# One inference step of a hybrid encoder layer: two dot or value half points in place of a whole point, 96 places of block 1 beside the mixers and 32 before them

## The chip, the cores and the metric

The kernel runs on one core of one Trainium2 chip. The metric is the device time of one execution in microseconds; lower is better.

## What is computed

One layer over nine blocks of 128 rows: block 0 holds 8 running streams of 16 frames, blocks 1 to 8 one new stream of 1024 frames. Cut to what matters:

```python
h = rmsnorm(x)                                        # D_MODEL = 1024
qa, ka, va, qb, kb, vb, rg, ga, gb = project(h)       # one product with w_in, 5888 columns
oa = softmax(qa @ ka + alibi, with sinks) @ va        # mixer A: 8 heads, own block and the one before
ob = norm(retention(qb, kb, vb, state)) * silu(rg)    # mixer B: 4 heads, state carried from block to block
x1 = x + (sigmoid(ga) * (oa @ w_a) + sigmoid(gb) * (ob @ w_b)) @ w_out
h2 = rmsnorm(x1)
q = h2 @ w_q; idx, gate = top16 of 128 x 128 product keys, for each of 8 heads
# 128 experts for each row, out of 16384; each has a row u and a row v of 1024 numbers
y = rmsnorm(x1 + sum_k gate_k * gelu(h2 . u[idx_k]) * v[idx_k])
```

The outputs are y of all rows, the newest keys and values, and the states.

## The kernel before

All is float32. **Stages** follow one another with a barrier between them, since each has buffers of its own.

1. The projection of blocks 0 and 1; the mixers of block 0; the mixers of block 1.
2. The projection stage. TensorE multiplies blocks 2 to 8 with the weights, in 16 tiles of columns; ScalarE scales each result into `zo` and stores it as `z_d`. Beside it VectorE searches the experts of blocks 0 and 1, and works off all 128 places of block 0 and the first `AHEAD` = 48 of block 1. A **place** is one expert for each of the 128 rows. It needs a gather of u rows (512 KB), a dot product with `h2` (one instruction over 1024 columns), later a gather of v rows and a weighted sum into the accumulator. The rows land in a ring of 16 slots; `ORDER1` is the order of 16 u or v rows each for block 1. At the end the accumulator is stored to `ac_d`.
3. The mixer stage, blocks 2 to 8. Beside the mixers VectorE works off the other places of block 1, here 80.
4. The last stage: the experts of blocks 2 to 8. Here u and v rows come with one gather, from a **table** `uv_d` of 16384 x 2048 numbers in memory. The kernel itself copies peer_u and peer_v into it, in 128 parts with two copies of 512 KB each (`pool_table`), by GpSimd's queue, at most two parts in flight: 24, 22 and 16 parts in stage 1, 20 ahead of the gathers in stage 2 (`TABLE_E` = 62 to `TABLE_S` = 82), and the other 46 in the mixer stage, two after each group of gathers from block 3 on.

**Order in the mixer stage.** Each engine has one list of instructions, written by hand, and works it off in order. Block `blk` is interleaved with the second half ("merge") of block `blk - 1`: its gate product, branch products, merge, output product, residual and norm. So `dve_block` (L666) gives for VectorE: gate product and gate biases of the block before (`dve_gate`, L418), `kdec`, `va`, then `qdT`, `qbT`, `kaT` out of the transposes, and only then can TensorE form the scores (L611); score sums (L689), soft-max, probabilities (L395, one instruction of 2048 columns), points 0 and 1, merge (`dve_merge`, L424), half of the transposed probabilities (L700), point 2, `oaT` (L703), norm of the retention (`dve_retention_norm`, L397), point 3, residual (L435), state, norm. TensorE (`pe_block`, L597): transposes of q and k, gated transposes (after the gate product), scores, branch products (L316, L319) after `atm`, transposes of the probabilities, mix transposes (L325, after the merge), attention and retention products, output product (L332), state product. It then waits for the norm before the next block. ScalarE (`act_block`, L646): Silu of the gate, copies, exponentials (L345, eight), sigmoids, copies, square and root.

**Points.** `dve_point(v, blk, j)` is a point: first the sum of three values of a group, then the dots of the group `PTS` = 4 later. There are three slots for u rows (`ru`) and three for v rows (`rv`), so GpSimd (L1485, L1493) asks for a group's rows only when VectorE has worked off the group before. Twelve places (`SET`) go through one Gelu on ScalarE. What is left after block 8 are the last set's values, here eight; they end in the norm of block 1, whose square and root stand on ScalarE ahead of its copies of the query products for block 2.

**SP's queue** carries all loads of the mixers, in this order in a block: values and keys of the next block, after mix transposes the gates, after the residual the x1 rows, after the norm the h2 rows, then the next x rows.

## Time and profile before

| | us |
|---|---|
| median of 3 runs (lowest, highest) | 4188.11 (4188.02, 4191.79) |
| the profiled execution | 4192.38 |
| its span, first to last instruction | 4190.6 |
| busy: TensorE, VectorE, GpSimd, ScalarE | 3301.8, 2487.3, 1817.5, 1049.8 |
| mixer stage, first load to the last stage's first load | 1168.56 to 1857.63 |
| gate products of blocks 2 to 8 | 1243.57, 1326.28, 1409.11, 1492.46, 1575.29, 1660.01, 1741.54 |

The shares over the span are an average over stages that have different limits, so they say little here. PE, DVE, ACT, POOL and SP are TensorE, VectorE, ScalarE, GpSimd and SyncE; a "q" behind the name is the engine's queue that issues DMAs. In a timeline each row has start, duration, engine, line of the kernel, operation, what is written and read, and, in brackets, how long the engine was idle before and what ended that. Durations of VectorE instructions one behind the other overlap a little, so starts are the better measure.

### The profile page before, as it was taken

Reading aid. Unit: us, or ns where it says so; the run is one execution under the profiler, and the core shown is the slowest. Engines: PE = TensorE matmul, PEld = TensorE weight load, DVE = VectorE, ACT = ScalarE, POOL = GpSimd, SP = SyncE. Lnnn points to the kernel's source line nnn. Section 1 sums busy time; section 2 is a strip of 40 time slices with the busy share of each in tenths; the row PEclk is TensorE's granted clock in tenths of the full one; section 3 lists DMA queues with packets and bytes.
Section 4 is the critical chain, followed back from the end, with each engine's and each line's share of the span. In section 5 each row is a group of like instructions: output and inputs, shape, how many; then the busy total and the mean of one; then the engine's idle time right before and its main releaser. Section 6 shows DMA issues by size and latency. Waiting matters only on the chain.

```text
span 4190.6 us, 32116 instructions
## 1 busy us (share of the span) xinstructions
PE 3301.8 (79%) x8957; PEld 1648.5 (39%) x8957; DVE 2487.3 (59%) x5001; ACT 1049.8 (25%) x2852; POOL 1817.5 (43%) x1668
## 2 busy tenths in 40 slices
PE   8776599999737676848878878878977977977776
PEld 5453256666424444423323333323433423422222
DVE  0122168988856676564775674684585585486444
ACT  2101011111112222212333333333333333323322
POOL 1020137787823443203444444444444444445554
PEclk9877799999958787979999999999999999999999
DMA  9888979999986888729999999999999999999998
GB/s 344 310 285 301 321 251 413 411 409 412 413 342 260 322 324 312 276 120 412 421 418 421 421 409 408 422 419 401 422 414 408 422 414 409 422 414 420 422 422 354
DMA packets 303583, 1563.02 MB, mean 373 GB/s; under 512 B 31280, under 2 KB 59184, under 8 KB 179888
## 3 DMA queue, kind: packets, MB, share of 16 engines
q0 software_dynamic: 239616, 1342.28, 80.2%
q1 hardware_dynamic: 49216, 197.92, 12.0%
q10 hardware_dynamic: 14592, 21.10, 1.3%
q8 instruction: 51, 0.84, 0.1%
q14 instruction: 108, 0.88, 0.1%
HBM read 1517.54 MB, written 179.04 MB: 405 GB/s over the span
## 4 chain that ended last, share of the span: by engine, by line
DMA 25%; PE 18%; issue 6%; DVE 4%; ACT 1%; POOL 1%; POOLq 0%; ACTq 0%; DVEq 0%
DMA ring<-uv_d,IXD_p 25%; PE ps L1778 15%; PE ps L1750 3%; DVE ring L1877 2%; ACT dg L1821 1%; POOL ring L1981 1%; DVE CA_p L967 0%; PE ps L1767 0%; DVE BV_p L957 0%; ACT GE_p L1815 0%; DVE II_p L1315 0%; DVE SC_p L1320 0%; DVE CA_p L1375 0%; DVE DOT_p L1877 0%; DVE ACC L1858 0%
## 5 line engine op out<-in xcount | busy, mean ns | idle before, releaser
L1778 PE MATMUL ps<-ring,dg 128*128 128x512 f32 x3584 | 1700.3, 613 | 477.2 <-ACT dg L1821 453.4
L1981 POOL DMA_INDIRECT ring<-uv_d,IXD_p x896 | 1071.7, 1196 | 1326.3 <-PE ps L1778 1077.3
L1877 DVE CUSTOM_DVE_ANT_0 ring<-ring,H 128x1024 f32<-128x1024 f32 x896 | 1094.0, 1223 | 906.4 <-DMA ring<-uv_d,IXD_p 885.5
L1778 PEld LDWEIGHTS ps<-ring,dg 128*128 128x128 f32 x3584 | 660.9, 193 | 1434.5 <-ACT dg L1821 721.9
L1216 PE MATMUL ps<-w,xg 128*128 128x368 f32 x1792 | 556.0, 473 | 2.0 <-ACT SC_s L914 2.0
L1815 ACT ACTIVATE GE_p<-DOT_p 128x2 f32<-128x2 f32 x448 | 91.1, 203 | 1494.9 <-DVE DOT_p L1877 1494.9
L1216 PEld LDWEIGHTS ps<-w,xg 128*128 128x128 f32 x1792 | 341.3, 191 | 216.3 <-ACT SC_s L914 2.2
L1821 ACT ACTIVATE dg<-gdi,GE_p 128x128 f32<-128x128 f32 x896 | 310.8, 394 | 48.9 <-ACT GE_p L1815 4.7
L1809 ACT ACTIVATE gdi<-ident,GD_p 128x128 f32<-128x128 f32 x896 | 303.2, 386 | 28.4 <-issue 21.4
L145 POOL DMA_DIRECT2D uv_d<-in_peer_u x128 | 68.4, 534 | 490.6 <-DMA uv_d<-in_peer_v 258.6
L1485 POOL DMA_INDIRECT rv<-in_peer_v,IXD x80 | 94.9, 1187 | 271.5 <-DVE AC L1467 252.2
L1750 PE MATMUL ps<-wq,hT_p 128*128 128x512 f32 x384 | 196.7, 594 | 0.0
L947 POOL DMA_INDIRECT ring_s<-in_peer_u,IXD_s x128 | 157.1, 1228 | 71.7 <-issue 37.8
L947 POOL DMA_INDIRECT ring_s<-in_peer_v,IXD_s x128 | 159.7, 1248 | 41.4 <-issue 38.4
L1079 DVE CUSTOM_DVE_ANT_0 ring_s<-ring_s,H_s 128x1024 f32<-128x1024 f32 x128 | 151.7, 1221 | 41.9 <-DMA ring_s<-in_peer_u,IXD_s 41.0
L226 PE MATMUL ps<-w,xg 128*128 128x368 f32 x512 | 160.0, 476 | 14.4 <-DMA w<-in_w_in 14.4
L1090 DVE SCALAR_TENSOR_TENSOR ACC_s<-ring_s,WG_s,ACC_s 128x1024 f32<-128x1024 f32 x126 | 157.1, 1289 | 14.0 <-DMA ring_s<-in_peer_v,IXD_s 13.8
L1245 ACT ACTIVATE zo<-ps,rstd 128x368 f32<-128x368 f32 x112 | 61.8, 566 | 371.9 <-PE ps L1216 370.9
L1467 DVE SCALAR_TENSOR_TENSOR AC<-rv,WG,AC 128x1024 f32<-128x1024 f32 x80 | 102.7, 1284 | 59.7 <-DMA rv<-in_peer_v,IXD 55.6
L1493 POOL DMA_INDIRECT ru<-in_peer_u,IXD x80 | 84.4, 1055 | 110.4 <-DVE DOT L1450 75.7
L1450 DVE CUSTOM_DVE_ANT_0 ru<-ru,H 128x1024 f32<-128x1024 f32 x80 | 96.6, 1223 | 56.5 <-DMA ru<-in_peer_u,IXD 56.3
L226 PEld LDWEIGHTS ps<-w,xg 128*128 128x128 f32 x512 | 98.0, 192 | 75.8 <-issue 15.6
(417 smaller groups left out, 2935.0 us busy)
## 6 DMA issues: line engine op xcount, KB each, us to landing
uv_d<-in_peer_u POOLq DMA_DIRECT2D x128, 512.0 KB, 6.5
uv_d<-in_peer_v POOLq DMA_DIRECT2D x128, 512.0 KB, 8.1
w<-in_w_in SPq DMA_DIRECT2D x8, 2944.0 KB, 15.3
w<-in_w_in SPq DMA_DIRECT2D x16, 1472.0 KB, 9.4
z_d<-zo ACTq DMA_DIRECT2D x16, 1288.0 KB, 18.6
ring<-uv_d,IXD_p POOLq DMA_INDIRECT x896, 11.2
gates_p<-z_d SPq DMA_DIRECT2D x7, 1536.0 KB, 10.0
wq_s<-in_peer_w_q SPq DMA_DIRECT2D x8, 1024.0 KB, 13.7
```

The lines of the kernel that those rows point to most:

```text
L226: mm = T.matmul(ps[:, m % AB, 0:WC], xg0[:, k, b * P:(b + 1) * P], w0[:, p % 2, n % 2, k, :], start=(k == 0), stop=(k == KT - 1))
L947: gather = g.indirect_dma_start(ring[:, n % RING, :], None, t["peer_u"] if kind == "u" else t["peer_v"], bass.IndirectOffsetOnAxis(ap=inde ...
L1079: V.tensor_tensor_reduce(out=row, in0=row, in1=H2[:], scale=1.0, scalar=0.0, op0=ALU.mult, op1=ALU.add, accum_out=DOT[:, k:k + 1]).then_in ...
L1090: V.scalar_tensor_tensor(ACC[:, k % 2], row, WG[:, k:k + 1], ACC[:, k % 2], ALU.mult, ALU.add).then_inc(d["freed"], 1)
L1216: mm = T.matmul(ps[:, n % AB, 0:WC], xg[:, k, b * P:(b + 1) * P], w[:, tile % 2, k, :], start=(k == 0), stop=(k == KT - 1))
L1467: V.scalar_tensor_tensor(AC1[:], row, WG1[:, k:k + 1], AC1[:], ALU.mult, ALU.add).then_inc(d["accz"], 1)
L1750: mm = T.matmul(bank(2 + n), hT[:, k, :], wq[:, k, n * 512:(n + 1) * 512], start=(k == 0), stop=(k == KT - 1))
L1778: mm = T.matmul(bank(6 + n), dg[:, k % DR, :], ring[:, k % RS, D + n * 512:D + (n + 1) * 512], start=(k == 0), stop=(k == NK - 1))
L1809: S.activation(gdi[:, k % GR, :], ident[:], ACT.Copy, scale=GD[:, k:k + 1]).then_inc(e["gdi"], 1)
L1821: S.activation(dg[:, k % DR, :], gdi[:, k % GR, :], ACT.Copy, scale=GE[:, k:k + 1]).then_inc(e["diag"], 1)
L1877: V.tensor_tensor_reduce(out=row, in0=row, in1=H2[:], scale=1.0, scalar=0.0, op0=ALU.mult, op1=ALU.add, accum_out=DOT[:, k:k + 1]).then_in ...
L1981: g.indirect_dma_start(ring[:, n % RS, :], None, uv_d, bass.IndirectOffsetOnAxis(ap=IXD[:, n:n + 1], axis=0)).then_inc(s_ring[n % RS], 16)
```

## The change

- `AHEAD` falls from 48 to 32 and `ORDER1` ends after 16 values less, so 32 places of block 1 are done in the projection stage and 96 in the mixer stage. `PTS` is 5: five groups of three in a block, `SET` is 15, and the last set has six places.
- `dve_point` is now half a point: even numbers are the values, odd ones the dots. The ten of a block are spread: values 0 before the score sums, dots 0 under the exponentials, three half points before the merge, three after it, two after the norm.
- `kaT`, `qbT` and `qdT` are made first in a block, before the gate product. The biases leave `dve_gate` and become `dve_biases`.
- The scaling of the probabilities (for blocks 1 to 8), the second half of the transposed probabilities and `oaT` go from VectorE to ScalarE.
- The table: `TABLE_S` is 88, so six more parts are copied by GpSimd in the projection stage, and the last 40 by SP, eight in each of blocks 3 to 7, two at a time, without a limit of their own (`rest_of_table`). GpSimd copies none in the mixer stage. The last stage waits for them with one more semaphore.
- Some semaphore increments that nobody waited for are gone.

```diff
 EARLY = 1
-TABLE_A, TABLE_BS, TABLE_E, TABLE_S = 24, 46, 62, 82
-AHEAD = 48
+TABLE_A, TABLE_BS, TABLE_E, TABLE_S = 24, 46, 62, 88
+AHEAD = 32
...
+        s_uvs = sem("uv_table_rest")
+
+        def rest_of_table(sp, lo, hi):
+
+            for part in range(lo, min(hi, NEXP // P)):
+                sp.dma_start(uv_d[part * P:(part + 1) * P, 0:D], rows(t["peer_u"], part)).then_inc(s_uvs, 16)
+                sp.dma_start(uv_d[part * P:(part + 1) * P, D:], rows(t["peer_v"], part)).then_inc(s_uvs, 16)
+
...
-            def dve_probs(v, blk, width):
+            def dve_probs(v, blk, width, scaled):
                 pr = Pr[:, :, 0:width]
                 v.wait_ge(s["exp"], blk + 1)
                 V.tensor_tensor(rs[:], rs[:], es[:], ALU.add).then_inc(s["den"], 1)
                 v.wait_ge(s["den"], blk + 1)
                 V.reciprocal(rs[:], rs[:]).then_inc(s["rden"], 1)
                 v.wait_ge(s["rden"], blk + 1)
-                V.tensor_tensor(pr, pr, rs[:].unsqueeze(2).to_broadcast([P, HA, width]), ALU.mult).then_inc(s["prob"], 1)
+                if scaled:
+                    V.tensor_tensor(pr, pr, rs[:].unsqueeze(2).to_broadcast([P, HA, width]), ALU.mult).then_inc(s["prob"], 1)
 
             def dve_retention_norm(v, blk, b0, step):
...
+            def dve_biases(v, blk):
+                v.wait_ge(s["z2"], 16 * blk + 16)
                 V.tensor_tensor(z(GA, 2 * D), z(GA, 2 * D), bg[:], ALU.add).then_inc(s["ga"], 1)
...
+            act.wait_ge(s["rden"], blk + 1)
+            for h in range(HA):
+                e = S.activation(Pr[:, h], Pr[:, h], ACT.Copy, scale=rs[:, h:h + 1])
+            e.then_inc(s["prob"], 1)
             if merge:
                 act_sigmoids(act, blk - 1)
             act.wait_ge(s["pt"], blk + 1)
-            S.activation(PT[:, 0:4].rearrange("p h c n -> p (h c n)"), bank(0, 2), ACT.Copy).then_inc(s["ptc"], 1)
+            for g in range(2):
+                S.activation(PT[:, 4 * g:4 * g + 4].rearrange("p h c n -> p (h c n)"), bank(2 * g, 2), ACT.Copy).then_inc(s["ptc"], 1)
             if merge:
                 act_mix(act, blk - 1)
+            act.wait_ge(s["oat"], blk + 1)
+            S.activation(oaT[:].rearrange("p j n -> p (j n)"), bank(0), ACT.Copy).then_inc(s["oatc"], 1)
             act_deviation(act, blk)
             if merge:
...
             step = Steps(v, s_vstep, STEPS_E if blk == 1 else STEPS_B + (blk - 2) * DVE_B)
+            v.wait_ge(s["t1"], blk + 1)
+            V.tensor_copy(qbT[:].rearrange("p h n -> p (h n)"), bank(1))
+            if blk <= 2:
+                v.wait_ge(s_tab, 32 * blk)
+            V.tensor_tensor(qdT[:].rearrange("p h n -> p (h n)"), bank(1), into[:].rearrange("p h n -> p (h n)"), ALU.mult)
+            V.tensor_copy(kaT[:, 1], ps[:, 3, 0:P]).then_inc(s["qkv"], 1)
+            if merge:
+                dve_gate(v, blk - 1)
+            wait_mixers(v, blk, half)
+            step.did(V.tensor_copy(va[:, 1], z(VA, P, half)))
+            for h in range(HB):
+                q = V.tensor_scalar(kdec[:, h, :], z(KB + h * DK, DK, half), outd[:, h:h + 1], None, ALU.mult)
+            q.then_inc(s["kdec"], 1)
             if merge:
                 if blk == 3:
                     v.wait_ge(s_bw, 16 * 8)
-                dve_gate(v, blk - 1)
-            wait_mixers(v, blk, half)
-            if blk <= 2:
-                v.wait_ge(s_tab, 32 * blk)
-            for h in range(HB):
-                q = V.tensor_scalar(kdec[:, h, :], z(KB + h * DK, DK, half), outd[:, h:h + 1], None, ALU.mult)
-            q.then_inc(s["kdec"], 1)
-            step.did(V.tensor_copy(va[:, 1], z(VA, P, half)))
-            v.wait_ge(s["t1"], blk + 1)
-            V.tensor_tensor(qdT[:].rearrange("p h n -> p (h n)"), bank(1), into[:].rearrange("p h n -> p (h n)"), ALU.mult)
-            V.tensor_copy(qbT[:].rearrange("p h n -> p (h n)"), bank(1))
-            V.tensor_copy(kaT[:, 1], ps[:, 3, 0:P]).then_inc(s["qkv"], 1)
-
+                dve_biases(v, blk - 1)
+
+            dve_point(v, blk, 0)
             if blk <= 2:
...
-            dve_probs(v, blk, 2 * P)
-            dve_point(v, blk, 0)
             dve_point(v, blk, 1)
+            dve_probs(v, blk, 2 * P, False)
+            for half_point in range(2, 5):
+                dve_point(v, blk, half_point)
             if merge:
                 dve_merge(v, blk - 1)
-            v.wait_ge(s["pt"], blk + 1)
-            V.tensor_copy(PT[:, 4:8].rearrange("p h c n -> p (h c n)"), bank(2, 2)).then_inc(s["ptc"], 1)
-            dve_point(v, blk, 2)
+            for half_point in range(5, 8):
+                dve_point(v, blk, half_point)
             v.wait_ge(s["oat"], blk + 1)
-            V.tensor_copy(oaT[:].rearrange("p j n -> p (j n)"), bank(0)).then_inc(s["oatc"], 1)
-
             V.tensor_copy(kaT[:, 0], kaT[:, 1])
-            V.tensor_copy(va[:, 0], va[:, 1]).then_inc(s["keep"], 1)
+            V.tensor_copy(va[:, 0], va[:, 1])
             dve_retention_norm(v, blk, 2, step)
-            dve_point(v, blk, 3)
+            for half_point in range(8, 10):
+                dve_point(v, blk, half_point)
             if merge:
...
-        ORDER1 = [("u", 0), ("u", 1), ("v", 0), ("u", 2), ("v", 1), ("v", 2)]
+        ORDER1 = [("u", 0), ("u", 1), ("v", 0), ("v", 1)]
...
-        PG, PTS = 3, 4
+        PG, PTS = 3, 5
...
-                grp = PTS * (blk - 2) + j
-                if blk > 2:
+                grp = PTS * (blk - 2) + j // 2
+                if j % 2:
+                    dve_expert_dots(v, grp)
+                elif blk > 2:
                     dve_expert_values(v, grp - PTS)
-                dve_expert_dots(v, grp)
 
...
+                        part = TABLE_S + 8 * (blk - 3)
+                        if blk > 2:
+                            rest_of_table(sp, part, part + 2)
+                            sp.wait_ge(s["prob"], blk + 1)
+                            rest_of_table(sp, part + 2, part + 4)
                         if blk == NB - 1:
...
+                            rest_of_table(sp, part + 4, part + 6)
+                            sp.wait_ge(s["ro"], blk + 1)
+                            rest_of_table(sp, part + 6, part + 8)
                             sp.wait_ge(s["x1"], blk)
                             sp.dma_start(rows(x1_d, blk - 1), X[:]).then_inc(s["x1st"], 16)
...
                             pool_dots(g, grp)
-                            if blk > 2:
-                                part = TABLE_S + 2 * (grp - PTS)
-                                pool_table(g, part, min(part + 2, NEXP // P))
                     for grp in range(LAST, TAIL):
...
-                        g.wait_ge(s_uv[i], 32 * (NEXP // P // 2))
+                        g.wait_ge(s_uv[i], 32 * (TABLE_S // 2))
                         g.sem_inc(d["pool"], 1)
+                    g.wait_ge(s_uvs, 32 * (NEXP // P - TABLE_S))
+                    g.sem_inc(d["pool"], 1)
                     with g.Fori(FB, NB) as blk:
```

## Rows read from the trace of the kernel before

**Rows 1.** Busy time by window: projection stage's end, block 4, block 8; window, us, engines, clock, DMA share, GB/s

```profile
1022.45:1130.34 107.89, 107.26 (x347) 65.56 (x346) 91.42 (x127) 17.34 (x34) 86.25 (x72) 1.00 1.03 411
1326.28:1409.11 82.83, 61.72 (x205) 37.42 (x205) 57.35 (x86) 19.34 (x35) 36.15 (x41) 0.81 0.81 309
1660.01:1741.54 81.53, 63.67 (x206) 37.96 (x207) 52.48 (x78) 20.14 (x35) 24.02 (x27) 0.82 0.77 286
```

**Rows 2.** Timeline, projection stage's end: start, us, engine, line, operation, count, idle before

```profile
1097.18 1.22 DVE L1128 CUSTOM_DVE_ANT_0 ring_s<-ring_s,SC_s 128x1024 f32<-128x1024 f32 x1
...
1130.34 0.37 ACTq L1248 DMA_DIRECT2D z_d<-zo  x1
...
1146.15 19.34 DVE L1139 SCALAR_TENSOR_TENSOR SC_s<-ring_s,WG_s,SC_s 128x1024 f32<-128x1024 f32 x14 [0.21 <-DMA ring_s<-in_peer_v,IXD]
...
1168.56 0.32 SPq L730 DMA_DIRECT2D zqk_p<-z_d  x1
```

**Rows 3.** DMA issues in 1125 to 1168: count, KB each, median us to landing

```profile
z_d<-zo ACTq DMA_DIRECT2D x1, 1288.0 KB, 15.2
...
ac_d<-SC_s SPq DMA_DIRECT2D x1, 512.0 KB, 2.6
```

**Rows 4.** Timeline of GpSimd, first and last table part of the stage, first gather

```profile
503.80 0.52 POOL L145 DMA_DIRECT2D uv_d<-in_peer_u  x1 [53.85 <-DMA w<-in_w_in]
...
572.05 0.52 POOL L145 DMA_DIRECT2D uv_d<-in_peer_u  x1 [1.49 <-DMA uv_d<-in_peer_v]
...
599.97 0.99 POOL L947 DMA_INDIRECT ring_s<-in_peer_u,IXD_s  x1 [26.90 <-DVE IXD_s L1045]
```

**Rows 5.** Waits of VectorE, 1168 to 1858: us in total, times, longest

```profile
DVE ru L1450 <- DMA ru<-in_peer_u,IXD: 56.3, 36, 8.3
DVE AC L1467 <- DMA rv<-in_peer_v,IXD: 55.6, 36, 9.1
```

**Rows 6.** Timeline of block 4, from its gate product to the next

```profile
1326.28 1.23 DVE L421 TENSOR_TENSOR gates_p<-gates_p,yn_p 128x1024 f32<-128x1024 f32 x1 [2.48 <-ACT gates_p L350]
...
1332.08 5.65 PE L611 MATMUL ps<-kaT,qaT_p 64*128 64x256 f32 x16 [2.54 <-DVE kaT L683]
...
1337.77 1.22 DVE L689 SCALAR_TENSOR_TENSOR Pr_p<-ps,alibi_p 128x1024 f32<-128x1024 f32 x1 [5.75 <-PE ps L611]
...
1340.78 9.30 PE L316 MATMUL ps<-wa_p,oaT_p 128*128 128x512 f32 x16 [1.04 <-DVE atm_p L692]
...
1347.59 0.17 DVE L391 TENSOR_TENSOR rs_p<-rs_p,es_p 128x8 f32<-128x8 f32 x1 [4.21 <-ACT Pr_p L345]
...
1349.91 13.90 PE L319 MATMUL ps<-wb_p,yT_p 128*128 128x512 f32 x32
...
1374.13 1.97 PE L325 MATMUL ps<-ident,gates_p 128*128 128x128 f32 x8 [8.58 <-DVE gates_p L430]
...
1384.40 13.90 PE L332 MATMUL ps<-wo_p,yT_p 128*128 128x512 f32 x32
...
1391.77 1.90 DVE L414 TENSOR_SCALAR yn_p<-ps,mv_p,sdv_p 128x256 f32<-128x256 f32 x4
...
1402.28 1.22 DVE L435 TENSOR_TENSOR X_p<-X_p,ps 128x1024 f32<-128x1024 f32 x1
...
1409.11 1.22 DVE L421 TENSOR_TENSOR gates_p<-gates_p,yn_p 128x1024 f32<-128x1024 f32 x1 [2.48 <-ACT gates_p L350]
```

**Rows 7.** DMA of 1326 to 1409: packets; issues with count, KB, us to landing

```profile
DMA packets 6649, 25.68 MB, mean 309 GB/s; under 512 B 737, under 2 KB 737, under 8 KB 6518
...
rv<-in_peer_v,IXD POOLq DMA_INDIRECT x12, 9.8
ru<-in_peer_u,IXD POOLq DMA_INDIRECT x12, 10.4
```

**Rows 8.** Timeline of the mixer stage's tail

```profile
1771.03 3.60 PE L1535 MATMUL ps<-wa_p,oaT_p 128*128 128x512 f32 x8
...
1777.41 1.01 ACT L1549 ACTIVATE zv_p<-ps 128x1024 f32<-128x1024 f32 x1
```

26 lines of the change are left out of this document (14 added, 12 removed).

## The prediction

> **What bounds the kernel now.** I first cut the span into stages with the busy time by window, then read in each stage what ends last. The projection stage ends in two parts: until 1130.34 us TensorE is busy for 107.26 of 107.89 us and the DMA engines are full (share 1.03, 411 GB/s) [rows 1]; there the last projection tile is stored. The stage nevertheless lasts until 1168.56, because VectorE still works off value rows of block 1 (fourteen in 19.34 us from 1146.15, so until 1165.5) and then stores the sum [rows 2]. So 38 us at its end belong to VectorE and its gathers alone.
>
> In the mixer stage nothing is full: in block 4, 82.83 us long, TensorE is busy 61.72, VectorE 57.35, and the DMA engines 0.81 of the time at 309 GB/s [rows 1]. That is a chain with holes in it. VectorE's waits name them: over the stage 56.3 us for dot rows and 55.6 us for value rows [rows 5]. The timeline of block 4 shows the others: 5.75 us for the score products, which started late at 1332.08 because all VectorE work since the gate product at 1326.28 stood ahead of kaT, and 4.21 for the exponentials [rows 6]. TensorE has a hole of its own: its mix transposes wait 8.58 us for VectorE's merge, because two whole points stand ahead of it [rows 6]. The last stage, 2333 us, is touched by no edit but one satisfied wait.
>
> **Projection stage.** The change removes 16 places, thus 16 dot rows and 16 value rows. After block 1's first 16 values, VectorE goes straight from 1097.2 into the last 16 values instead of 16 dots [rows 2]. At 1.38 us for a value (19.34/14, rows 2), whose rows can be there as the dot rows were, that ends at 1097.2 + 22 = 1119; the 512 KB sum then takes 2.6 [rows 3]. What is late next is the store of the last projection tile, issued at 1130.34. Before it landed after 15.2 us, with gathers at full rate around it [rows 3]; without them I size it from the 512 KB store: 1288 KB is 2.5 times the bytes, so 2.5 x 2.6 = 6.5 at most. The next stage then begins at 1137 instead of 1168.6: **-32**. Ends: -36 (landing 2.6), -23 (landing 15.2 as now).
>
> Six more table parts come ahead of the gathers. The 20 parts now are issued from 503.80 to 572.05, 3.6 us each, and GpSimd then waits 26.90 us for the places of block 0 [rows 4]. Six parts are 6 x 3.6 = 22 us: they fit, with 5 us left, in which their last rows (8 us to land, an estimate from two parts in flight) may still be in the queue. Cost on VectorE 0 to 3 us; it has 1130 - 1122 = 8 us of slack. I take nothing. If that cover were gone, 22 us would go onto VectorE and 14 beyond the slack.
>
> **Blocks 1 and 2** have no merge. Scaling the probabilities moves from one VectorE instruction to eight on ScalarE; no row shows that form. The nearest is eight exponentials of the same 256 columns, for which VectorE waits 4.21 [rows 6]; without their sums it may be half, so 2 to 4.2, and I take 3, against 2.3 for what it replaces (2048 columns; a dot over 1024 goes every 1.14, rows 2). And the two transposed halves are now copied one after the other (+1). Against that kaT is made ahead of kdec, with only into awaited (-1.5). Block 1: +0.5 (-1 to +3). Block 2 has five dot groups instead of four, one more round trip, partly under the norm: +1 (-2 to +6).
>
> **Blocks 3 to 7.** I lay out one block from its gate product (t = 0), with the durations of block 4 [rows 6]; a half point D is three dots, 3.5 us (1.22 each, slightly overlapped, rows 2); V is three values, 4.0. All now depends on one number, the time L from the release of a group of slots to the landing of its first row, which I carry as a variable. Median from issue to landing is 9.8 (values) and 10.4 (dots) in this block [rows 7].
> - From the gate product to the scores' start VectorE now works 5.8 us. The three copies that the scores need, 1.5 by their 1152 columns, now go ahead of the gate, into the wait for the Silu: t = 4.3. V0 until 8.3. TensorE meanwhile: gated transposes until 3.3, scores 5.65 until 8.9. They no longer wait for kaT, which is done before the gate (2.5 us earlier), and VectorE's 5.8 us wait is filled with V0.
> - Scores to soft-max maxima 5.6 (1337.77 to 1347.59 less the 4.21): 14.6. D0 until 18.1 lies under the exponentials (18.8). Denominator: 19.3.
> - V1 until 23.3 (its rows were asked for at 8.3). D1 was released at 18.1, so from 18.1 + L. V2 from 23.3 + L.
> - TensorE: branch products start at atm, 11.9, and take 9.2 + 13.7 = 22.9 (1340.78 to 1363.6): 34.8. ScalarE's scaling (19.3 + 4.2 at most) and sigmoids lie under them; without that cover it would cost as much as in block 2. Merge not before 34.8 and not before V2's end.
> - With L = 9: D1 27.1 to 30.6, V2 32.3 to 36.3, merge until 39.9, D2 until 43.4, V3 45.3 to 49.3, D3 52.4 to 55.9, norm 5.4 (it ends at 1393.67 now, begun when the third point was done) until 61.3, V4 until 65.3, D4 until 68.8. TensorE after the merge: 10.3 (1374.13 to 1384.40) and 13.9 for the output product, which ends at 64.1 and is not last. Residual at 68.8; from there to the next gate 6.83 as now (1402.28 to 1409.11). **Period 75.6**.
> - The same with L = 6 gives 71.2 (TensorE's chain is then last), 8 gives 73.3, 10 gives 79.2, 12 gives 86.8.
> - VectorE's busy time goes from 57.4 by 7.5 (three more places) minus 4 (3584 columns moved to ScalarE, 1.14 per 1024) to 61, no bound. DMA: 25.68 MB [rows 7] plus six gathers of 0.52 are 28.8 MB, at 411 GB/s 70 us, no bound above 71.
>
> Which L? For less: the eight table parts of a block leave GpSimd's queue, in which gathers stood behind four 512 KB copies at a time (2.1 MB, 5 us). For more: 28.8 MB in 75.6 us are 381 GB/s instead of 309, 0.93 of full. Low end 6 (a group of 1.57 MB at 411 GB/s is 3.8, plus 2 of latency), high end 12. I take 9, nearer to today's 10.
>
> Here a rule stands against the change. In the row, copies and gathers together reach the same 411 GB/s at share 1.03 [rows 1], so no queue has bandwidth of its own. The Trainium skill, DMA: Bandwidth & Descriptors, "Issuing engines are not separate DMA queues", says so too: transfers interleave on the same 16 engines whoever issues them. By that alone L stays at 10 and the sum is 22 us smaller. The same page, "Queues, rings and completion order", lets each engine alternate between queues packet by packet; by that a gather no longer stands behind a whole copy, and L would be 8. No row here shows gathers beside copies from SP.
>
> SP's queue: the parts are issued after kdec, after prob, after the gates' load and after ro. Behind the first two stands the gates' load (at mixt, t = 42, wanted at 73: 31 us for 10 of transfer); behind the last the x1 store at 69, 18 us later. An issue costs 0.3 [rows 2]. ScalarE's gated copy waits for the h2 store, which goes out about 1 us before the next gate; landing after ten, it is there at 9, and the branch products want the copy at 11.9. Nothing.
>
> Blocks 3 to 7: 5 x (82.8 - 75.6) = **-36** (L = 6: -58; L = 10: -18).
>
> **Block 8** has no table and only two groups of dots; now 81.53 [rows 1]. Its chain is TensorE's, residual at 64, and 8.5 to the gate: 73, **-8.5** (-12 to -3).
>
> **Tail.** Six values instead of eight. ScalarE's query copies wait behind the norm of block 1 until 1777.41, and the query transposes for them. TensorE has its queries at 1771.03 and a 3.60 us product to do first [rows 8]; it could transpose at 1774.6, and now does 1 us after the first copy, at 1778.5: **-4** (-8 to 0).
>
> **Sum.** -32 + 0.5 + 1 - 36 - 8.5 - 4 = -79. The profiled execution took 4192.4 (span 4190.6 and 1.8 around it): 4113. The median of the runs is 4.3 below it: 4188.1 - 79 = **4109**.
>
> **Rivals.** (a) TensorE's chain is last and gathers vanish behind it, L at most 7: 22 us more and some of the outer ends, 4072 to 4092. For it: 0.19 of DMA time is idle in a block. Against: the gathers ask in bursts. 0.15. (b) The waits for rows come back in five round trips instead of four, L of 10.5 to 12: period 81 to 87, so 4137 to 4177. For it: 112 us of such waits now and a load that rises to 0.93. 0.20. (c) Slower: the same five trips with L of 13 or more, because copies from SP take turns with every gather. A dot group then costs 16.5, period 91, six blocks +49 against -35 from the rest: about 4202. It decides from a period of 89 on. 0.05. (d) The projection stage doesn't end sooner, as the last tile's store or late gathers hold it: +9 to +22 on the forecast, inside the range; it alone turns no sign. (e) The half points lie as described, but the merge is still late because V2 is; that is in the layout (39.9 against 38.5).
>
> **Chances.** Forecast case (L 7 to 10.5, 4092 to 4137) 0.58, (a) 0.15, (b) 0.20, (c) 0.05, between (b) and (c) 0.02. 0.2% is 8 us, about what a measurement of this kernel can tell from no change. Faster 0.93, same 0.02, slower 0.05. Range: from (a)'s 4075 to 4150, the upper ends of the sum with L = 10 and the first part of (b).
>
> **What would show it.** The mixer stage starts near 1137, after the tile's store, not after VectorE. VectorE's wait before the score sums falls from 5.8 to under 1; the wait before the mix transposes falls below 6; gathers land after 7 to 10; gate products are 74 to 78 apart. I am wrong if landing rises beyond 12, if periods stay over 81, or if first gathers of the projection stage are late by more than 8.

## The result, and the profile after

| | before | after |
|---|---|---|
| median (lowest, highest) of 4 runs | 4189.64 (4188.02, 4191.79) | 4155.20 (4148.77, 4157.13) |
| after / before, 95% interval | | 0.9915 (0.9898 to 0.9932) |
| span of the profiled execution | 4190.6 | 4151.9 |
| first load of the projection stage | 460.80 | 456.06 |
| length of the projection stage | 707.8 | 672.2 |
| block 2, from the first load to its gate product | 75.0 | 83.2 |
| mean period of blocks 3 to 7 | 83.3 | 83.4 |
| block 8 | 81.5 | 76.2 |
| tail, to the next stage's first load | 116.1 | 108.7 |
| last stage | 2333.0 | 2338.4 |

The change gains 34 us, 0.8%. The forecast was 79 us, and its range ended at 4150. The projection stage gives what was forecast. The five blocks that were to give 36 us give nothing. In the two profiled executions the parts are -4.7 (start of the projection stage), -35.5, +8.2 (block 2), +0.6 (blocks 3 to 7), -5.4 (block 8), -7.4 (tail) and +5.4 (last stage).

Busy time by window of the kernel after: window, us, the five engines, granted clock, DMA share, GB/s. The lines answer to [rows 1].

```profile
1022.45:1128.30 105.85, 99.43 (x322) 60.80 (x320) 74.50 (x91) 15.37 (x28) 60.15 (x52) 0.99 0.88 349
...
1295.06:1378.42 83.36, 61.27 (x205) 37.03 (x205) 60.59 (x92) 24.16 (x45) 31.88 (x30) 0.81 0.95 349
1628.62:1704.79 76.17, 63.22 (x206) 37.49 (x207) 48.68 (x72) 24.97 (x45) 18.76 (x18) 0.84 0.66 234
```

Block 4 (second line) is as long as before, with VectorE at 60.6 us as forecast (61), but the DMA share went from 0.81 to 0.95. The projection stage's end in its timeline, and the landing of its last tile from the DMA issues of 1115 to 1131 (count, KB, us), beside [rows 2, 3]:

```profile
1110.00 4.06 DVE L1161 SCALAR_TENSOR_TENSOR SC_s<-ring_s,WG_s,SC_s 128x1024 f32<-128x1024 f32 x3
...
1122.51 0.37 ACTq L1270 DMA_DIRECT2D z_d<-zo  x1
...
1128.30 0.32 SPq L751 DMA_DIRECT2D zqk_p<-z_d  x1
```

```profile
z_d<-zo ACTq DMA_DIRECT2D x1, 1288.0 KB, 5.0
```

VectorE is done at 1114, then the last tile's store is awaited, which lands after 5.0 us instead of 15.2. Block 4 in the timeline, to be laid beside [rows 6]:

```profile
1295.06 1.23 DVE L429 TENSOR_TENSOR gates_p<-gates_p,yn_p 128x1024 f32<-128x1024 f32 x1 [1.09 <-ACT gates_p L358]
...
1303.92 1.23 DVE L711 SCALAR_TENSOR_TENSOR Pr_p<-ps,alibi_p 128x1024 f32<-128x1024 f32 x1 [0.34 <-PE ps L623]
...
1313.75 0.23 DVE L399 TENSOR_TENSOR rs_p<-rs_p,es_p 128x8 f32<-128x8 f32 x1 [0.78 <-ACT Pr_p L353]
...
1318.56 1.23 DVE L1472 CUSTOM_DVE_ANT_0 ru<-ru,H 128x1024 f32<-128x1024 f32 x1 [0.22 <-DMA ru<-in_peer_u,IXD]
...
1320.81 1.22 DVE L1472 CUSTOM_DVE_ANT_0 ru<-ru,H 128x1024 f32<-128x1024 f32 x1 [1.02 <-DMA ru<-in_peer_u,IXD]
...
1328.04 1.28 DVE L1489 SCALAR_TENSOR_TENSOR AC<-rv,WG,AC 128x1024 f32<-128x1024 f32 x1 [4.73 <-DMA rv<-in_peer_v,IXD]
1331.44 2.67 DVE L1489 SCALAR_TENSOR_TENSOR AC<-rv,WG,AC 128x1024 f32<-128x1024 f32 x2 [2.12 <-DMA rv<-in_peer_v,IXD]
...
1350.48 1.22 DVE L1472 CUSTOM_DVE_ANT_0 ru<-ru,H 128x1024 f32<-128x1024 f32 x1 [5.44 <-DMA ru<-in_peer_u,IXD]
...
1353.00 1.23 DVE L1472 CUSTOM_DVE_ANT_0 ru<-ru,H 128x1024 f32<-128x1024 f32 x1 [1.28 <-DMA ru<-in_peer_u,IXD]
...
1355.45 1.23 DVE L1472 CUSTOM_DVE_ANT_0 ru<-ru,H 128x1024 f32<-128x1024 f32 x1 [1.22 <-DMA ru<-in_peer_u,IXD]
...
1366.35 1.23 DVE L1472 CUSTOM_DVE_ANT_0 ru<-ru,H 128x1024 f32<-128x1024 f32 x1 [1.04 <-DMA ru<-in_peer_u,IXD]
...
1368.84 1.23 DVE L1472 CUSTOM_DVE_ANT_0 ru<-ru,H 128x1024 f32<-128x1024 f32 x1 [1.26 <-DMA ru<-in_peer_u,IXD]
...
1370.44 1.23 DVE L1472 CUSTOM_DVE_ANT_0 ru<-ru,H 128x1024 f32<-128x1024 f32 x1 [0.36 <-DMA ru<-in_peer_u,IXD]
...
1378.42 1.23 DVE L429 TENSOR_TENSOR gates_p<-gates_p,yn_p 128x1024 f32<-128x1024 f32 x1 [1.09 <-ACT gates_p L358]
```

```profile
1337.69 1.97 PE L333 MATMUL ps<-ident,gates_p 128*128 128x128 f32 x8 [5.98 <-DVE gates_p L441]
```

```profile
1341.88 1.21 POOL L1516 DMA_INDIRECT ru<-in_peer_u,IXD  x1 [3.43 <-DVE DOT L1472]
1343.39 1.08 POOL L1516 DMA_INDIRECT ru<-in_peer_u,IXD  x1 [0.30 <-issue]
```

The waits before the score sums (0.34 for 5.75) and for the exponentials (0.78 for 4.21) are nearly gone, and the wait before the mix transposes fell from 8.58 to 5.98, as laid out. Then read the fourth group of dots: its first row is asked for at 1341.88 and used at 1350.48, 8.6 us later, but the second and third follow 2.5 us apart, while a dot takes 1.2 and GpSimd asked for them 1.5 us apart. All of VectorE's waits for rows in this block, and the DMA issues of the block (issues, KB each, us to landing), beside [rows 7]:

```profile
DVE ru L1472 <- DMA ru<-in_peer_u,IXD: 11.9, 8, 5.4
DVE AC L1489 <- DMA rv<-in_peer_v,IXD: 6.8, 2, 4.7
```

```profile
DMA packets 7586, 29.07 MB, mean 349 GB/s; under 512 B 846, under 2 KB 846, under 8 KB 7455
...
uv_d<-in_peer_u SPq DMA_DIRECT2D x8, 512.0 KB, 11.3
uv_d<-in_peer_v SPq DMA_DIRECT2D x8, 512.0 KB, 13.8
...
rv<-in_peer_v,IXD POOLq DMA_INDIRECT x15, 9.0
ru<-in_peer_u,IXD POOLq DMA_INDIRECT x15, 8.9
```

The forecast's layout held 10.5 us of such waits (3.8 + 1.7 + 1.9 + 3.1); the block has 18.7. The 8.2 us between them match the 7.8 us between the periods. By the brackets above, 11.4 us are waits for the first row of a group (0.22, 4.73, 5.44 and 1.04), near the 10.5 of the layout; the other 7.3 us are waits for a second or third row, of which the layout has none. The medians from issue to landing, 9.0 and 8.9, are about the L = 9 assumed, though the forecast counts L from the release: the third group's last dot ended at 1341.07, so there it was 9.4.

### The profile page after: what moved, and what is told of

Read it like the earlier page. It is cut to its first block, busy times and chain, and to the rows that moved or that the text cites. A ratio compares the mean times of both kernels' runs of the same rounds, so it can differ in the third digit from the quotient of the medians.

```text
span 4151.9 us, 32152 instructions
## 1 busy us (share of the span) xinstructions
PE 3300.1 (79%) x8957; PEld 1646.0 (40%) x8957; DVE 2455.2 (59%) x4976; ACT 1088.9 (26%) x2931; POOL 1752.2 (42%) x1588
## 3 DMA queue, kind: packets, MB, share of 16 engines
q0 software_dynamic: 228096, 1300.34, 78.5%
## 4 chain that ended last, share of the span: by engine, by line
DMA 26%; PE 18%; issue 7%; DVE 4%; ACT 1%; POOL 1%; POOLq 0%; ACTq 0%; DVEq 0%
DMA ring<-uv_d,IXD_p 26%; PE ps L1807 14%; PE ps L1779 3%; DVE ring L1906 2%; ACT dg L1850 1%; POOL ring L2012 1%; ACT GE_p L1844 0%; DVE BV_p L979 0%; DVE BP_p L984 0%; DVE CA_p L989 0%; PE ps L1796 0%; DVE CA_p L1397 0%; DVE DOT_p L1906 0%; DVE VV_p L1332 0%; DVE ACC L1887 0%
## 5 line engine op out<-in xcount | busy, mean ns | idle before, releaser
L145 POOL DMA_DIRECT2D uv_d<-in_peer_u x88 | 45.7, 519 | 502.9 <-DMA uv_d<-in_peer_v 268.8
L1516 POOL DMA_INDIRECT ru<-in_peer_u,IXD x96 | 102.5, 1068 | 222.0 <-DVE DOT L1472 160.2
L1472 DVE CUSTOM_DVE_ANT_0 ru<-ru,H 128x1024 f32<-128x1024 f32 x96 | 115.6, 1222 | 105.7 <-DMA ru<-in_peer_u,IXD 105.6
L1489 DVE SCALAR_TENSOR_TENSOR AC<-rv,WG,AC 128x1024 f32<-128x1024 f32 x96 | 123.2, 1284 | 54.7 <-DMA rv<-in_peer_v,IXD 48.6
L226 PEld LDWEIGHTS ps<-w,xg 128*128 128x128 f32 x512 | 98.1, 192 | 75.6 <-issue 15.5
```

What stands on the lines that cost most here:

```text
L226: mm = T.matmul(ps[:, m % AB, 0:WC], xg0[:, k, b * P:(b + 1) * P], w0[:, p % 2, n % 2, k, :], start=(k == 0), stop=(k == KT - 1))
L1489: V.scalar_tensor_tensor(AC1[:], row, WG1[:, k:k + 1], AC1[:], ALU.mult, ALU.add).then_inc(d["accz"], 1)
```

## Experiments

All numbers of a row come from its profiled execution; "period" is the mean of blocks 3 to 7. A ratio is given where the kernel was timed against the kernel before on its chip. A ratio compares within one set; totals of different sets are not comparable, since in some TensorE stopped in the projection stage and the mixer stage began up to 80 us later (last experiment).

| kernel | groups | parts in a block | period | block 2 | mixer stage starts | ratio to before (95%) |
|---|---|---|---|---|---|---|
| before | 4 | 8 | 83.3 | 75.0 | 1168.6 | |
| after | 5 | 8 | 83.4 | 83.2 | 1128.3 | 0.9915 (0.9898, 0.9932) |
| e7_before_copies_after | 4 | 0 | 79.5 | 74.9 | 1174.8 | |
| e1_copies_after | 5 | 0 | 72.5 | 83.4 | 1178.2 | |
| e4_copies_in_tail | 5 | 4 | 77.9 | 83.2 | 1192.8 | 0.9934 (0.9897, 0.9972) |
| e2_copies_early | 5 | 8 | 80.1 | 83.3 | 1197.8 | 0.9941 (0.9903, 0.998) |
| e3_copies_gpsimd | 5 | 8 | 81.5 | 81.9 | 1135.2 | |
| e6_whole_points | 5 | 8 | 93.3 | 84.8 | 1132.9 | |
| e5_four_groups | 4 | 8 | 74.0 | 72.5 | 1164.7 | |
| e11_four_no_copies | 4 | 0 | 68.7 | 72.9 | 1165.1 | |
| e8_row_release | 5 | 8 | 79.5 | 82.4 | 1130.5 | 0.9849 (0.9833, 0.9866) |
| e13_release_early | 5 | 8 | 78.5 | 83.9 | 1188.4 | |
| e10_four_combined | 4 | 4 | 68.3 | 81.2 | 1165.1 | 0.9791 (0.9776, 0.9806) |
| e9_combined | 5 | 3 | 73.2 | 82.8 | 1128.9 | 0.978 (0.9766, 0.9793) |
| e12_combined_b8 | 5 | 2 | 71.3 | 80.5 | 1133.5 | 0.9771 (0.9756, 0.9786) |
| e14_sixteen | 5 | 16, 16, 8, 0, 0 | 87.4, 87.1, 90.1, 70.8, 71.6 | 84.4 | 1196.2 | |
| e15_changed_again | 5 | 8 | 82.8 | 83.1 | 1203.3 | 1.0015 (0.9987, 1.0044) |
| e16_combined_again | 5 | 2 | 70.6 | 84.4 | 1208.8 | 0.9731 (0.9662, 0.9801) |

In the expectations A is the theory that the DMA engines are full by the bytes of a block, B that copies collide with the gathers that the chain awaits, and C that the copies are innocent and the fifth round trip is all. Later ones are D (copies in flight share the engines with the gathers, and part of that lies on the chain of round trips), S (copies from SP take turns with every gather, copies from GpSimd would harm less) and F (A in a new form: full DMA engines are the floor of a block).

**Are the copies the cause?** The 40 parts of blocks 3 to 7 go behind the mixer stage, onto GpSimd's queue ahead of the last stage; the same with the 46 parts of the kernel before.

```diff
-                            rest_of_table(sp, part, part + 2)
...
+                    pool_table(g, TABLE_S, NEXP // P)
                     for i in range(2):
-                        g.wait_ge(s_uv[i], 32 * (TABLE_S // 2))
+                        g.wait_ge(s_uv[i], 32 * (NEXP // P // 2))
```

> The changed kernel with the 40 table parts of blocks 3 to 7 taken out of SP's queue; GpSimd copies them in one piece after the mixer stage, ahead of the first gather of the last stage, at 3.4 to 3.6 us a part (about 140 us more there). What is read is the distance of the gate products of blocks 3 to 7, 83.4 us with the copies. Theory A (a copied part takes all DMA engines for 3.4 us, not the 2.5 that its bytes would take at the rate of gathers; eight of them and the block's gathers fill 78 of 83 us): 73 to 76. Theory B (the copies only come at the wrong time, bunched beside the last gathers of a block): also 73 to 76. Theory C (five round trips of the two groups of slots cost it, copies or not): 80 or more. Time: A and B about 4250, C about 4290.

> The kernel before with its 46 parts taken out of the mixer stage and copied in one piece ahead of the last stage (about 160 us more there). What is read is the distance of the gate products, 83.3 with the copies. It has four whole points in a block and its DMA engines were busy 0.81 of the time. Theories A and B: its 11.5 us of waits for rows shrink to 3 to 6, so 76 to 79. Theory C: the waits are round trips, 81 or more. If it comes to the same as the changed kernel without copies, the new order in the block is worth only the fifth group.

Without copies the changed block takes 72.5 us, 11 less, and the block before 79.5, only 4 less. C falls for the changed kernel (it wanted 80 or more); the 79.5 lie between the ranges, A and B had 76 to 79 and C 81 or more. Block 4 of the first, in the busy time by window and in VectorE's waits for rows (us in total, times, longest):

```profile
1332.97:1405.67 72.70, 60.72 (x205) 36.80 (x205) 60.49 (x92) 24.16 (x45) 32.01 (x30) 0.83 0.80 279
```

```profile
DVE ru L1472 <- DMA ru<-in_peer_u,IXD: 5.7, 2, 4.2
DVE AC L1489 <- DMA rv<-in_peer_v,IXD: 1.3, 2, 1.0
```

The waits fall from 18.7 to 7.0: those for a first row from 11.4 to 4.2, those for later rows from 7.3 to 2.9. The fourth group of dots, asked for at 1375.70, 1377.20 and 1378.59, thus as far apart as with copies, comes in 1.3 us apart instead of 2.5:

```profile
1383.07 1.23 DVE L1472 CUSTOM_DVE_ANT_0 ru<-ru,H 128x1024 f32<-128x1024 f32 x1 [4.20 <-DMA ru<-in_peer_u,IXD]
...
1384.33 1.23 DVE L1472 CUSTOM_DVE_ANT_0 ru<-ru,H 128x1024 f32<-128x1024 f32 x1
```

The new order of work is thus worth about what was forecast, as long as nothing else is moved: 79.5 to 72.5 with a group more.

**How much for a part, and where?** Four parts in each of blocks 3 to 8, one at each place, and 16 in the tail; or all eight of a block early, four behind kdec and four behind the probabilities.

```diff
-                            rest_of_table(sp, part, part + 2)
+                            rest_of_table(sp, part + 0, part + 1)
...
+                    rest_of_table(sp, TABLE_S + PARTS_BLK * (NB - 3), NEXP // P)
                     sp.wait_ge(s["x1"], NB)
```

> The changed kernel with four parts in each of blocks 3 to 8, one at each of the four places, and the last 16 after the last query weights in the tail of the mixer stage, where the DMA engines are busy 0.24 of 109 us. Theory A: four parts are 14 us of DMA time less in a block, DMA is no longer the bound, blocks 75 to 78, block 8 at most 3 more, the tail 0 to 4 more (16 parts are 56 us in a hole of 80): time 4115 to 4130. Theory B: two thirds of it, 4130 to 4140. Theory C: 4150 to 4160.

> The changed kernel with all eight parts of a block in its first part: four after kdec and four after prob, none after the mix transposes or after ro. Theory A (DMA time is full whatever the order): 80 to 84 us a block, time within 10 of 4155. Theory B (placement): no copy stands beside the last two groups of dots, 76 to 78 us a block, time about 4123. Theory C: 83, 4155.

72.5, 77.9 and 83.4 us for 0, 4 and 8 parts: 1.4 us each, with no bend. Early places give 3.3 us. B falls: it had 76 to 78 for early places, and they give 80.1. A's own ranges, 75 to 78 and 80 to 84, hold both numbers; against it speaks the even price, since a floor of 78 us by bytes lies 14 us lower with four parts less and would have hidden the first four. Theory D takes their place. The 16 parts in the tail cost it 1 us (110.0 for 108.7), since its DMA engines were nearly idle, as the window of the kernel after shows (share 0.24):

```profile
1704.79:1813.52 108.73, 71.00 (x203) 34.19 (x202) 73.94 (x232) 18.14 (x20) 2.82 (x3) 0.84 0.24 96
```

**Is it SP's queue?**

```diff
                             pool_dots(g, grp)
+                            if blk > 2 and j < 4:
+                                part = TABLE_S + 8 * (blk - 3) + 2 * j
+                                pool_table(g, part, min(part + 2, NEXP // P))
```

> The changed kernel with its 40 last table parts back on GpSimd's queue, two behind each of the first four groups of gathers in blocks 3 to 7, at most two parts in flight. Theory D (copies in flight share the DMA engines with the gathers and lie on the chain of round trips, whoever issues them): gate products of blocks 3 to 7 are 81 to 86 us apart, as 83.4 with SP's copies or a little more. Rival S (copies from SP take turns with every gather, and in GpSimd's queue they would do less harm): 79 or less.

81.5 us, 2 less than with SP, so S falls (it had 79 or less). The queue, the limit of two parts in flight and the places change together here, and all three are worth 2 us, hardly more than the 1.3 us by which block 2, without parts in both kernels, differs; most of the price stays with the transfers themselves.

**Half points or whole ones?**

```diff
-            dve_point(v, blk, 0)
...
-            for half_point in range(2, 5):
+            for half_point in range(0, 4):
```

> The changed kernel with its half points put back into whole points (values and dots together) at five places of a block: the first behind the probabilities, two before the merge, one after it, one after the norm. If the spread of half points is what pays for the fifth group: the waits before score sums and exponentials come back and the merge is later, gate products 88 to 93 apart. Rival (only the number of groups and the copies count): 83 to 85 apart.

93.3 us. In block 4 VectorE again waits 4.5 us for the scores and 4.2 for the exponentials, and TensorE 9.1 for the merge. The half points pay 10 us a block; with whole ones the change would be a loss (one execution, 4218.96 us, beside 4193.93).

**What does the fifth group cost?** AHEAD 48 and four groups again, in the new layout; then the same without copies.

```diff
-AHEAD = 32
+AHEAD = 48
...
-        PG, PTS = 3, 5
+        PG, PTS = 3, 4
```

> The changed kernel with AHEAD 48 and four groups of places a block, in the new half-point layout and with the same copies from SP. Theory D (the fifth round trip of a block costs what copies and layout gain): gate products of blocks 3 to 7 77 to 80 us apart, block 2 75 to 77 long, but the projection stage some 35 us longer, so the total is 4150 to 4175 beside 4155. Rival (the layout itself gains nothing, whatever the count of groups): 82 to 84 apart, total 4185 or more.

> Four groups a block (AHEAD 48) in the new layout, with the last 40 table parts copied behind the mixer stage. It is the fourth corner beside the changed kernel (five groups, eight parts, 83.4 us a block), five groups without copies (72.4) and four groups with eight parts (74.0). In the last, the merge still waits 6.6 us for VectorE, which waits for value rows. If the chain of round trips is what copies lengthen, that wait goes here and TensorE's chain remains: 67 to 71. If a block has a floor of 72 by TensorE and VectorE anyway: 71.5 to 74, and then copies alone or the fifth group alone are hidden and only both together cost.

Four groups with all eight parts take 74.0 us a block, below the 77 to 80 expected, and 72.5 in block 2: 10 us less than five groups in each, 58 in six blocks, where the projection stage loses 36. Its single run, 4133.66 us, stands beside a kernel before of 4193.93 (median of 7) on the same chip, so this kernel, with less changed, does more than the change. Together the four corners are, in us a block:

| | no parts | eight parts |
|---|---|---|
| four groups | 68.7 | 74.0 |
| five groups | 72.5 | 83.4 |

The group alone costs 3.8 us, the parts alone 5.3, both 14.7: they aren't additive. The landings point to why. Four groups without parts, then with eight: a block's window, and its gathers with count and median us to landing.

```profile
1376.20:1444.83 68.63, 59.95 (x205) 35.47 (x205) 53.19 (x84) 24.17 (x45) 24.72 (x24) 0.88 0.73 251
```

```profile
rv<-in_peer_v,IXD POOLq DMA_INDIRECT x12, 5.5
ru<-in_peer_u,IXD POOLq DMA_INDIRECT x12, 5.8
```

```profile
1387.07:1460.20 73.13, 59.90 (x205) 36.25 (x205) 53.28 (x83) 24.15 (x45) 24.03 (x24) 0.85 0.93 340
```

```profile
rv<-in_peer_v,IXD POOLq DMA_INDIRECT x12, 9.2
ru<-in_peer_u,IXD POOLq DMA_INDIRECT x12, 9.8
```

A row lands after 5.5 us without copies and after 9.5 with them. With four trips 5.3 us a block come of these 4 us each, with five 10.9: the fifth leaves less room to hide them.

**Is the chain of trips the limit, or the DMA engines?** GpSimd asks for each row when its own slot is free and not when the group's three are:

```diff
-                if grp:
-                    g.wait_ge(d["accz"], BASE_V + grp * PG)
                 for k in places(grp):
+                    if grp:
+                        g.wait_ge(d["accz"], BASE_V + k - PG + 1)
```

> The changed kernel, but GpSimd asks for each row as soon as its own slot is free, and not when the whole group of three is: the first row of a group is asked for 2.4 us earlier, in ten round trips of a block. Theory D (the chain of round trips from a slot's release to its landing sets the period): 77 to 80.5 us apart in blocks 3 to 7, total 15 to 30 us less than the changed kernel. Rival F (the DMA engines at share 0.95 are the floor of the block): 82 or more apart, total within 5 us.

79.5 us, 4 less with the same bytes, and 0.9849 of the kernel before. D had 77 to 80.5, F 82 or more: the chain sets the period. But the engines are close behind (their share over blocks 4 to 7 is 0.97): with the early places added, and with sixteen parts a block, the runs were these.

> The changed kernel with rows asked for one by one and the eight parts of a block issued four behind kdec and four behind the probabilities. Alone, the first brought 83.4 down to 79.5 and the second to 80.1. Theory F (a floor of 78 by the DMA engines): 77.5 to 79, that is nothing more from the second. Rival D (chain only): both add up, 75.5 to 76.5.

> The changed kernel with rows asked for one by one, and the same 40 parts at the same four places, but four at a time instead of two: sixteen in block 3, sixteen in block 4, eight in block 5 (in its first two places), none in blocks 6 and 7. From copies alone at 287 GB/s with share 0.94 in stage 1 of the kernel before, a part needs 3.4 us of all DMA engines, and the rest of a block 50 us. Theory F (DMA engines full: a floor of 78 with eight parts): 100 to 108 for a block with sixteen. Rival D (1.4 us a part, as between 0, 4 and 8 parts, however many): 89 to 93. Blocks 6 and 7, without parts: 70 to 72.5 by both.

The first took 78.5 us: the two savings of 3.9 and 3.3 don't add up, which F had said (77.5 to 79) and D had not (75.5 to 76.5). The second took 87.4, 87.1, 90.1, then 70.8 and 71.6 us without parts. Its windows of blocks 3 to 6:

```profile
1280.58:1367.98 87.40, 61.56 (x205) 37.02 (x205) 60.58 (x93) 23.28 (x43) 31.46 (x30) 0.79 0.98 375
1367.98:1455.05 87.07, 62.05 (x205) 37.21 (x205) 60.67 (x93) 24.16 (x45) 32.18 (x30) 0.79 1.01 400
1455.05:1545.10 90.05, 60.97 (x205) 36.47 (x205) 60.12 (x93) 24.15 (x45) 32.75 (x30) 0.78 0.97 366
1545.10:1615.90 70.80, 59.93 (x205) 35.43 (x205) 60.05 (x92) 24.16 (x45) 34.54 (x30) 0.86 0.81 286
```

Here the engines are full (0.97 to 1.01), and parts of the first two blocks spill into the third. So a single block says little about the price of sixteen; the three together hold 40 parts in 264.5 us. Less 3 x 50.3 for all other bytes (20.7 MB at 411 GB/s) that is, as an estimate, 2.8 us a part, not 3.4. F's prices would make it 287 us and its 100 us a block fall; D's 89 to 93 a block are nearer, though two of the three lie below. By the 2.8, eight parts have a floor of about 50.3 + 8 x 2.8 = 73 us. Neither theory foretold all of this. (The window from which F took its 3.4 us, shown further below, lies in stage 2, not in stage 1.) What holds the last kernels at 78.5 between that floor and their chain stays open.

**Do the findings add up to a better kernel?** Rows asked for one by one, and fewer parts in blocks 3 to 7: four groups with four parts (16 in the tail); five groups with three (22 in the tail); five groups with two and eight in block 8 (22 in the tail).

```diff
-                        part = TABLE_S + 8 * (blk - 3)
+                        part = TABLE_S + 2 * (blk - 3)
...
-                            rest_of_table(sp, part, part + 2)
+                            rest_of_table(sp, part + (0 if blk == NB - 1 else 0), part + (2 if blk == NB - 1 else 1))
...
+                    rest_of_table(sp, TABLE_S + 18, NEXP // P)
```

> Four groups a block (AHEAD 48), rows asked for one by one, four table parts in each of blocks 3 to 8 and 16 in the tail. By the theory: 69 to 72 a block, the projection stage as with AHEAD 48 (mixer stage from 1165), tail 110: 4110 to 4122. Rival (a floor near 74): 4130 or more.

> The changed kernel with rows asked for one by one, three table parts (behind kdec, behind the probabilities, behind the gates' load) in each of blocks 3 to 8 and the other 22 in the tail. By the theory (79.5 a block with row release, 1.4 less for each of five parts taken out): 72 to 74 a block, the tail 110 to 114: 4100 to 4108, faster than any other kernel here. Rival (22 parts don't fit the tail, whose transfers are the query weights): the gain comes back behind the tail, 4120 or more.

> As the one before, but two parts in each of blocks 3 to 7 and eight in block 8, which has only two groups of dot rows; again 22 in the tail. If a part costs 1.2 to 1.4 us in blocks 3 to 7 and less in block 8: 71.5 to 73 a block, block 8 74 to 78, total 4095 to 4105, at most 5 us less than the kernel before it. If a part costs the same in block 8, it is the same or slower.

Medians 4104.96, 4098.85 and 4093.87 us beside 4191.55. All three are 1 to 5 us below the ranges expected. The last has the lowest median, 0.9771 of before, but its executions (4090.74 to 4099.15) overlap those of the second (4094.91 to 4102.76), so these two are not told apart. Its windows of blocks 3 to 7, block 8 and the tail:

```profile
1214.01:1570.29 356.28, 301.69 (x1025) 181.94 (x1025) 300.17 (x461) 119.95 (x219) 168.27 (x150) 0.85 0.85 308
1570.29:1641.53 71.24, 62.38 (x205) 37.20 (x206) 48.25 (x72) 24.96 (x45) 20.27 (x18) 0.86 0.96 359
1641.53:1753.46 111.93, 72.85 (x204) 34.89 (x203) 73.94 (x232) 18.14 (x20) 3.41 (x3) 0.84 0.90 306
```

Block 8 takes its eight parts and is 71.2 us long, the tail its 22 parts for 3 us more than the kernel after. Only block 2 resists, at 80 to 83 us, with 10 MB of weights beside its gathers. There, once rows are asked for one by one, they are no longer the limit. With four groups it took 72.5 us in e5_four_groups and takes 81.2 in e10_four_combined, though VectorE waits 17.1 us for rows instead of 26.9; then it stands still at the end of the block:

```profile
1244.87 0.69 DVE L689 COPY qbT_p<-ps 128x512 f32<-128x512 f32 x1 [20.02 <-PE ps L308]
```

TensorE in turn waits for block 3's queries and keys (`zqk_p`), which SP issues only at 1218.62, after the weights, and which are there at 1241.8.

**How much of the gain rests on the projection stage?**

> The changed kernel itself, once more, beside the kernel before. In six runs the mixer stage began at 1175 to 1198 us instead of 1130 to 1135, since TensorE stopped for 25 to 41 us in the projection stage (its waits there name nothing that released it, and its last tile came at 1169 to 1187 instead of 1122 to 1130). In the kernel before the same stop of 25 us moved the mixer stage by only 6 us, since VectorE ends the stage there. If such stops occur here, the changed kernel is 0 to 0.3% faster; if not, 0.8% as at first. Blocks 3 to 7 take 83 to 84 us each in both cases.

> The kernel with rows asked for one by one, two parts in each of blocks 3 to 7, eight in block 8 and 22 in the tail, once more. Its gain over the changed kernel lies in the mixer stage alone: 52 to 65 us less than the changed kernel here, whatever the projection stage does.

In this set the changed kernel took 4229.58 us (12 runs) beside 4218.38 (17 runs): 1.0015, 0.9987 to 1.0044, no gain, where 0 to 0.3% was expected. The kernel before lost 29 us against its first median too, the changed one 74; this set has no profile of the kernel before. Its mixer stage was as before (682.6 us long, 685.2 at first; periods 81.8 to 83.3), but began at 1203.34. The changed kernel's busy time by window, TensorE's wait and the last tile:

```profile
600.00:700.00 100.00, 75.26 (x212) 42.11 (x211) 73.66 (x116) 7.98 (x14) 77.21 (x72) 0.83 1.00 392
700.00:800.00 100.00, 91.12 (x278) 54.58 (x279) 98.46 (x233) 10.48 (x21) 70.30 (x57) 0.93 1.00 384
```

```profile
PE ps L1238 <- issue: 43.3, 43, 2.3
```

```profile
1197.56 0.37 ACTq L1270 DMA_DIRECT2D z_d<-zo  x1
```

TensorE stops 43 times between products, for 43.3 us, with a granted clock of 0.83 and 0.93 (means over 100 us, between its levels of 1.2 and 2.4 GHz; 1.00 in both windows at first), and the last tile is 75 us late; so is the whole rest. The stops are 43 of these 75 us; between 600 and 900 us a product also takes 334 ns on average instead of 309. "Issue" names no releaser, and what stops TensorE is not shown. One rival is open: the profile lists a DMA queue for instructions in this stretch, and no view says whether they came late beside the full engines. The engines were full in the first execution as well (share 1.03), so that alone isn't the cause. The kernel before meets such stops too; in e7_before_copies_after, which has its projection stage, the same two views read:

```profile
PE ps L1216 <- issue: 24.8, 28, 2.5
```

```profile
1169.33 0.37 ACTq L1248 DMA_DIRECT2D z_d<-zo  x1
```

Its last tile is 39 us late, but the stage ends only 6 us late (1174.8 for 1168.6), since 38 us of VectorE's work stood behind the last tile in that kernel; here the tile's store is only just last. The combined kernel had the stops as well (mixer stage from 1208.78). Its ratio of 0.9731 (0.9662 to 0.9801) comes from the two fastest of its four executions; the median of all four, 4140.11 us, is 0.981 of the kernel before. Its mixer stage is 619.2 us long, 63 less than the changed kernel's beside it (52 to 65 expected).

## Why the prediction was wrong, point by point

- **Projection stage, -32.** Measured -35.5, right, and by the named step: the last tile's store, 5.0 us for the 6.5 assumed. That the last tile was issued 666.5 us into the stage instead of 669.5 was not forecast. What the step missed is what VectorE's 38 us had been covering: they hid late ends of TensorE, which [rows 1] could not show in an execution that had none. With the stops of the last set the gain is gone. Rival (d), at +9 to +22 and "alone turns no sign", named this place and was far too small.
- **Blocks 0 and 1, +0.5.** The projection stage's first load came 4.7 us earlier (456.06). In the other runs it lies at 454.6 to 459.8 us with the changed kernel's stage 1 and at 458.75 with that of before (e7_before_copies_after), so most of the 4.7 may be chance.
- **Block 2, +1 (-2 to +6).** Measured +8.2. With a group's rows released together, five groups cost 10 us more there than four, with and without table parts in the later blocks (83.2 and 83.4 for 72.5 and 72.9). I let the fifth trip hide partly under the norm. In the timeline three groups wait in full, as this one:

```profile
1192.93 1.23 DVE L1472 CUSTOM_DVE_ANT_0 ru<-ru,H 128x1024 f32<-128x1024 f32 x1 [9.24 <-DMA ru<-in_peer_u,IXD]
```

- **Blocks 3 to 7, -36.** Measured +0.6, the whole miss. The order on VectorE and TensorE came out as laid out. The step that failed is VectorE's wait for rows: the layout gives it 10.5 us a block, and it was 18.7. In the layout a group's rows land as fast as VectorE takes them, so that only the first is awaited; beside eight parts of copies the later ones came up to 2.5 us (values once 3.4) apart and cost 7.3 us of waits. L, 9.4 from the release where 9 was taken, adds about 1 us by the layout itself. A second term erred in the same direction: "DMA 28.8 MB at 411 GB/s, 70 us, no bound above 71" took the rate of gathers for copies from memory to memory. [rows 4] said 3.6 us for a part of 1.05 MB; this window of the kernel before, with copies nearly alone, says 287 GB/s at share 0.94:

```profile
505.00:560.00 55.00, 48.69 (x150) 25.45 (x149) 25.98 (x146) 7.91 (x7) 15.14 (x30) 0.97 0.94 287
```

  By that the floor is 8.39 MB at 305 and 20.7 at 411, 78 us, and the forecast of 75.6 stood below it. The sixteen parts correct this to about 73, so the floor itself was not what held the block at 83.4; but it leaves the engines 2 to 3 us of slack in 75.6, and the forecast took five bursts of gathers to stay short in it.
- **The sum at L = 10.** The text calls it 22 us smaller; by its own line (-18 for -36 in blocks 3 to 7) it is 18.
- **The rivals.** (b), five round trips with a period of 81 to 87 and 4137 to 4177 us, is what happened, at 83.4 and 4155; its reason, a load that rises, was right, but its L of 10.5 to 12 did not occur, so its number is partly luck. It had 0.20 where the forecast had 0.58. (e) held: the merge is late because of the values, and begins 39.0 us after the gate product instead of 36.3. (c) did not occur, but "slower" was nearer than its 0.05: the last set lies around no change, by a mechanism that no rival held.
- **The rule of the Trainium skill**, DMA: Bandwidth & Descriptors, "Issuing engines are not separate DMA queues", was the better guide: with the copies moved between SP and GpSimd the period differs by 2 us, without them by 11. The alternation packet by packet in "Queues, rings and completion order", on the same page of the Trainium skill, would fit the rows that land 2.5 us apart beside copies (no run here isolates it); it was read as a gain for the first row, and would be a loss for the third.
- **Block 8**, -8.5: measured -5.4. **Tail**, -4: measured -7.4. Both inside their ends. The last stage, taken as untouched, is 5 us longer; why is open.

## What to carry to other kernels

A block's transfers belong in two sums: bytes at the rate of their own kind, and round trips at the landing time that the total load gives. When a change both adds a trip and moves bytes beside it, try the two apart: here either alone cost 4 to 5 us a block and both 15. When one wait is shortened, read which load the next step waits for: in block 2 it was the one issued behind the weights. Bytes without a due time go where the DMA share is low (here the tail at 0.24 and block 8), and an engine that ends a stage late may be covering another one whose time varies from run to run.

## What the runs showed of the hardware

- Copies from memory to memory ran at 287 GB/s at a DMA share of 0.94 nearly alone (505 to 560 us of the kernel before); a stretch of mostly gathers ran at 411 at 1.03 [rows 1]. Beside gathers a part of 1.05 MB took 2.8 us of full engines, an estimate from e14_sixteen.
- With eight parts beside them, gathers of 512 KB landed after 9.2 to 9.8 us (e5_four_groups) instead of 5.5 to 5.8 (e11_four_no_copies); with two parts and five groups after 6.8 to 6.9 (e12_combined_b8).
- In some executions TensorE stopped 25 to 55 us in total (24.8 in e7_before_copies_after, 55.3 in e16_combined_again) in a stretch where the DMA engines were full, in products that waited for nothing the profile names. One and the same chip had sets with and without such stops.
